# Pads between buffers: every main matmul's moving operand 288 bytes past its weights, modulo 512

## The reference

```python
for l in range(DEPTH):
    h = hybrid_mixer(x, w_in[l], ...);            x = layer_norm(alpha * x + h, ...)
    h = memory_cross_attention(x, mem, ...);      x = layer_norm(alpha * x + h, ...)
    h = conv_ffn(x, ffn_w_in[l], ...);            x = layer_norm(alpha * x + h, ...)
```

## Time and profile before

| | |
|---|---|
| Median of 3 runs | 2807.03 us (2804.65 to 2807.98) |
| Profiled execution | 2804.18 us |
| Its span, first to last instruction | 2802.4 us |
| TensorE busy (PE), weight loads (PEld) | 2721.5 us, 2499.1 us |
| VectorE, ScalarE, GpSimd busy | 2108.0 us, 1693.9 us, 71.8 us |
| Read from HBM | 675.32 MB, 243 GB/s over the span |
| Mean granted TensorE clock | 0.987 of full speed |

### The profile page before, as it was taken

How to read it: one execution, slowest core, us unless ns; L and a number is a source line. 1 busy time by engine, 2 the same in 40 slices (tenths; PEclk the granted TensorE clock), 3 DMA queues, 4 the chain that set the end, 5 groups by cost and what they waited for, 6 DMA issues and landing times.

```text
span 2802.4 us, 42816 instructions
## 1 busy us (share of the span) xinstructions
PE 2721.5 (97%) x18410; PEld 2499.1 (89%) x18418; DVE 2108.0 (75%) x2088; ACT 1693.9 (60%) x1856; POOL 71.8 (3%) x114
## 2 busy tenths in 40 slices
PE   7999999999999999999999999999999999999998
PEld 6999999999999989989999999888888888888886
DVE  5777647876667658767577667688898989888896
ACT  4555536654555546645577654677777777677675
POOL 1100000001000000000000000000000000000000
PEclk9999999999999999999999989999999999999999
DMA  7545447745536457634588733698988989898894
GB/s 237 170 147 166 154 159 257 268 141 170 157 121 196 151 181 268 229 96 136 187 296 299 256 93 106 244 371 339 379 340 339 377 344 372 335 382 338 340 373 182
DMA packets 304403, 679.22 MB, mean 242 GB/s; under 512 B 16560, under 2 KB 238032, under 8 KB 261072
## 3 DMA queue, kind: packets, MB, share of 16 engines
q1 hardware_dynamic: 288832, 617.67, 61.5%
q0 software_dynamic: 15376, 58.75, 6.4%
HBM read 675.32 MB, written 4.69 MB: 243 GB/s over the span
## 4 chain that ended last, share of the span: by engine, by line
PE 79%; DVE 10%; ACT 8%; issue 2%; DMA 1%; SPq 0%; ACTq 0%; DVEq 0%
PE bank L550 75%; DVE ew_lo L1871 4%; ACT ring_tail L2058 3%; ACT w_hi L1989 2%; DVE ring_low L1362 1%; PE bank L1166 1%; DMA ring_head<-in_w_in 1%; PE bank L630 1%; DVE std L1295 1%; PE bank L590 1%; DVE ring_tail L1319 0%; DVE ring_low L1282 0%; PE bank L669 0%; DVE xT L1616 0%; ACT ew_hi L2342 0%
## 5 line engine op out<-in xcount | busy, mean ns | idle before, releaser
L1871 DVE TENSOR_TENSOR ew_lo<-ring_head,ew_hi 128x2048 fp32r<-128x2048 f32 x336 | 759.3, 2287 | 41.5 <-ACT ew_hi L2342 41.5
L2342 ACT CAST ew_hi<-ring_head 128x2048 fp32r<-128x2048 f32 x336 | 640.6, 1915 | 223.9 <-PE bank L550 223.8
L550 PE MATMUL bank<-xs_hi,ring_low 128*128 128x256 f32 (+1 forms) x2608 | 511.9, 283 | 0.0
L550 PEld LDWEIGHTS bank<-xs_hi,ring_low 128*128 128x128 f32 (+1 forms) x2608 | 414.1, 190 | 1.5 <-issue 0.7
L550 PE MATMUL bank<-ew_hi,xe_hi 128*128 128x512 f32 x896 | 353.2, 394 | 0.0
L550 PE MATMUL bank<-ew_hi,xe_lo 128*128 128x512 f32 x896 | 349.3, 390 | 0.0
L550 PE MATMUL bank<-ew_lo,xe_hi 128*128 128x512 f32 x896 | 348.7, 389 | 0.0
L550 PE MATMUL bank<-x_hi,w_hi 128*128 128x256 f32 x1152 | 322.0, 287 | 13.5 <-ACT x_hi L2050 7.7
L550 PE MATMUL bank<-x_hi,ring_low 128*128 128x256 f32 x1152 | 316.6, 281 | 0.0
L1362 DVE TENSOR_TENSOR ring_low<-ring_head,w_hi 128x2048 fp32r<-128x2048 f32 x105 | 240.0, 2289 | 101.1 <-ACT w_hi L1989 101.1
L550 PE MATMUL bank<-x_lo,w_hi 128*128 128x256 f32 x1080 | 296.9, 281 | 0.0
(11 more groups left out here) (430 smaller groups left out, 5497.7 us busy)
## 6 DMA issues: line engine op xcount, KB each, us to landing
ring_head<-in_moe_w_gate SPq DMA_DIRECT2D x112, 1024.0 KB, 7.2
ring_head<-in_moe_w_up SPq DMA_DIRECT2D x112, 1024.0 KB, 7.0
ring_head<-in_moe_w_down SPq DMA_DIRECT2D x112, 1024.0 KB, 7.1
ring_head<-in_w_in SPq DMA_DIRECT2D x82, 1024.0 KB, 5.4
ring_tail<-in_ada_w POOLq DMA_DIRECT2D x48, 1024.0 KB, 10.0
ring_head<-in_ffn_w_in SPq DMA_DIRECT2D x44, 1024.0 KB, 6.4
ring_head<-in_ffn_w_out SPq DMA_DIRECT2D x22, 1024.0 KB, 8.7
ring_head<-in_xa_kv SPq DMA_DIRECT2D x16, 1024.0 KB, 5.4
```

What stands on the lines that cost most here:

```text
L550: ins = nc.tensor.matmul(out, lhsT, rhs, start=start, stop=stop, **kw)
L1871: v.tensor_tensor(ew_lo[:, h, :], ring(c % 6), ew_hi[:, h, :].bitcast(F32), ALU.subtract).then_inc(w_used[c % 6], 1)
L2342: a.copy(ew_hi[:, (e * len(PARTS) + c) % DEPTH_HI, :], ring(c % 6)).then_inc(f.count(part_hi), 1)
```

## The change

Eight pads are declared between buffers, `SKEW` = 56 floats (224 bytes) or `SKEW_BACK` = 72 floats (288 bytes). No instruction, no size and no order changes. The starts modulo 512 become:

| Buffer | before | after |
|---|---|---|
| ring_low, ring_head, xT, work, memT, ye, back, kb, gates | 128 | 128 |
| xs_hi, xs_lo | 416 | 416 |
| chunk_high | 416 | 128 |
| qa, qb, hc, mem, out (high and low), mixer buffers | 416 | 416 |
| w_hi | 416 | 128 |
| x_hi, x_lo, act_hi, act_lo | 416 | 416 |
| ew_hi, ew_lo | 416 | 416 |
| xe_hi, xe_lo, eact_hi, eact_lo | 416 | 128 |

```diff
--- before.py
+++ after.py
@@ -42,6 +42,7 @@
 MIXER_CHUNKS = 16
 NARROW = 40
 DT_AT = 32
+SKEW, SKEW_BACK = 56, 72
 class Follow:
 
 
@@ -204,26 +205,34 @@
         with ExitStack() as loads:
             with ExitStack() as twin:
                 xs = [in_scope(twin, n, KD, TOK, dt=F32R) for n in ("xs_hi", "xs_lo")]
+                skew_chunk = in_scope(twin, "skew_chunk", SKEW)
                 chunk_high = in_scope(twin, "chunk_high", CH, dt=F32R)
             ring_tail = in_scope(loads, "ring_tail", SLOTS - 6, CH)
+            skew_loads = in_scope(loads, "skew_loads", SKEW)
             with ExitStack() as twin:
+                skew_q = in_scope(twin, "skew_q", SKEW_BACK)
                 _, qb_hi, qb_lo, _, hc_hi, hc_lo, qa_hi, qa_lo = (in_scope(twin, n, k, TOK, dt=F32R) for n, k in (
                     ("under_q", 12), ("qb_hi", 4), ("qb_lo", 4), ("under_v", 12), ("hc_hi", 4), ("hc_lo", 4), ("qa_hi", 4), ("qa_lo", 4)))
             with ExitStack() as twin:
+                skew_mem = in_scope(twin, "skew_mem", SKEW_BACK)
                 _, mem_hi, mem_lo = (in_scope(twin, n, k, TOK, dt=F32R) for n, k in (("under_mem", 32), ("mem_hi", KD), ("mem_lo", KD)))
             with ExitStack() as twin:
+                skew_out = in_scope(twin, "skew_out", SKEW_BACK)
                 _, out_hi, _, out_lo = (in_scope(twin, n, k, TOK, dt=F32R) for n, k in (
                     ("under_out", 44), ("out_hi", 4), ("between_out", 4), ("out_lo", 4)))
             with ExitStack() as mixer:
+                skew_mixer = in_scope(mixer, "skew_mixer", SKEW_BACK)
                 qa, ka, qb, gb, gc, hc = (in_scope(mixer, n, 4, TOK) for n in ("qa", "ka", "qb", "gb", "gc", "hc"))
                 va, vb = (in_scope(mixer, n, 2, 512) for n in ("va", "vb"))
                 qhalf = [[in_scope(mixer, f"qhalf{a}{m}", 4, TOK) for m in range(2)] for a in range(2)]
                 probsT = in_scope(mixer, "probsT", 2, 2, 2, TOK)
             with ExitStack() as ffns:
                 w_hi = in_scope(ffns, "w_hi", DEPTH_HI, CH, dt=F32R)
+                skew_x = in_scope(ffns, "skew_x", SKEW_BACK)
                 x_hi, x_lo = (in_scope(ffns, n, KD, TOK, dt=F32R) for n in ("x_hi", "x_lo"))
                 act_hi, act_lo = (in_scope(ffns, n, 2, 2, TOK, dt=F32R) for n in ("act_hi", "act_lo"))
         ew_hi, ew_lo = (sb(n, DEPTH_HI, CH, dt=F32R) for n in ("ew_hi", "ew_lo"))
+        skew_xe = sb("skew_xe", SKEW)
         xe_hi, xe_lo = (sb(n, KD, P, dt=F32R) for n in ("xe_hi", "xe_lo"))
         eact_hi, eact_lo = (sb(n, ETILES, P, dt=F32R) for n in ("eact_hi", "eact_lo"))
 
```

## The result

The changed kernel takes 2824.44 us (median of 4 runs, 2820.72 to 2827.03), the kernel before 2807.09 (4 runs, 2804.65 to 2807.98). The ratio is 1.0062, with a 95% interval of 1.0047 to 1.0077: slower by some 17 us, where 15 us faster was forecast, and outside the range of 2775 to 2806.

The account below looks back on a forecast made before the run. The prediction took a stream of TensorE matmuls, whose spacing sets the time, as the bound, except in the wide feed-forward. Gains of 3.2 + 1.7 + 10.5 = 15.4 us gave 2791.5 us as likeliest, range 2775 to 2806.

Parts of the forecast that it names:

- The chunks of 256 columns: Straight 256-column matmuls: mixed distances to all 288 saves 1.06 ns each; turned ring_low chunks keep 118.3 ns.
- Term 3: Experts: 4032 matmuls of 512 columns gain 3.2 ns each, 12.9 us, less 2.4 at changes of expert: 10.5 us.
- the rival that ended on the slower side: Experts: streams meet their weights later, 3.0 ns a matmul on top of today's pitch, 2814 us; chance 6%.
- 216 ns: Rival in the experts: matmuls fall to the pitch of bf16 products with unchanged weights, 2766 us; chance 12%.
- Term 1: Dense feed-forwards: 3168 matmuls gain 1.06 ns each, times 0.95, 3.2 us; the wide one gives nothing.
- The share of 0.95: TensorE's share of the chain in layer 1's dense feed-forward (94.7%), used to scale the gain of Term 1.
- Term 2: Mixers and cross attention, chunks with hi in chunk_high: 2016 matmuls gain 1.06 ns each, times 0.80, 1.7 us.
- VectorE and ScalarE: Their operations at the new addresses: VectorE's subtraction at no cost, ScalarE's casts put at nothing.

Follow-up runs that it names:

- e1: The changed kernel without its last pad, before xe, so the experts are back at distance 0: 2804.24 us, ratio 0.9992 to the kernel before.
- m1: Also m1_map: a kernel of its own, only groups of 48 fp32r matmuls at 89 settings; 512 columns took 226.9 ns at distance 0, 233.1 at 288.
- e2: The kernel before with the pad before xe alone (224 bytes): 2825.50 us, ratio 1.0078.
- e4: The kernel before with a pad of 256 bytes before xe: 2806.01 us, ratio 1.0005.
- e5: The kernel before with a pad of 192 bytes before xe (distance 64 modulo 256): 2813.00 us, ratio 1.0024.
- e3: The changed kernel with straight 256-column products at distance 192 modulo 256 and experts back at 0: 2792.20 us, ratio 0.9953 to the kernel before.
- e8: The same kernel as e3, measured once more: 2796.45 us, ratio 0.9966.
- e7: As e3, but the dense feed-forwards' w_hi, x and act lie as in the kernel before: 2796.33 us, ratio 0.9959.
- m3_map_columns: A kernel of its own, only matmul groups of 64 to 512 columns, narrower weights and bf16; 512 columns with 32-column weights: 11.11 us at 0, 10.89 at 32.

## Why the prediction was wrong, step by step

- **The chunks of 256 columns**: right in the rows above. From 116.8 and 117.9 ns to 116.6 in the chain, and the turned ones unchanged. Distance 32 is cheaper than 0 there, and that is not a property of the buffers. But 116.6 is one of two spacings: the changed kernel has stretches at 117.8 ns too, in the feed-forward of layer 2 from 1137 to 1157 us, and e1 has them through all of that feed-forward. The prediction took one row for the whole stage.
- **Term 3, the experts: the failed step.** It says "The excess hardly grows with the columns: it goes with the change of weights, once per matmul. So I take the same 3.2 ns". The first half was read at distance 0 alone, where it is true (13.3 and 13.8 ns), and carried over to a distance at which only 256 columns had been seen. There it is false: 10 ns at 256 columns, 20 at 512. The 3.2 ns gained became 6.2 ns lost: 4032 x 6.2 = 25.0 us, of which 21 show. The difference fits the wait at the change of expert: before, loads of weights waited 4.6 us in all for xT, seven times (the row below); after, that wait is gone. m1, e2, e4 and e5 show the term, alone and in the kernel, at distances 0, 288, 256 and 320 modulo 512.

```profile
PEld bank L1166 <- DVE xT L1616: 4.6, 7, 0.7
```

- **The pads were named modulo 512**; the period is 256. That changed nothing here, since both residues are 32 modulo 256, but the search has half the room.
- **The bounds.** No row offered a price above 227.1 ns at 512 columns, and the rival that ended on the slower side was priced from turned chunks, 3.0 ns on top of today's: 2814, at 6%. It was right in sign and in that the loss comes with the longer stream, had half the size (3.0 for 6.2 ns), and too small a chance; its mechanism is neither shown nor refuted. An unknown whose one end had no row above it deserved a range open upwards: 216 ns was taken seriously below, nothing as far above.
- **Term 1, the feed-forwards, 3.2 us:** at most 0.7 us came in layer 1, where it said 1.6, and nothing in layer 2. The share of 0.95 was read from the chain, which says who was last, not by how much. From the first to the last start of x_hi with w_hi, layer 1 takes 176.7 us before, 176.0 in the changed kernel, 176.7 in e1 with the same pads, 176.8 in e3; layer 2 takes 176.8 before and 177.0 in the changed kernel. These are layer 1's rows of before and of e3:

```profile
L550 PE MATMUL bank<-x_hi,w_hi x352: 278/281/551, 424.9 to 601.6; 128*128 128x256 f32 x176
```
```profile
L559 PE MATMUL bank<-x_hi,w_hi x352: 276/281/582, 422.1 to 598.9; 128*128 128x256 f32 x176
```

  Two things take the gain. One is waiting. TensorE's line had 94.7% of this stage; in the changed kernel, from 460 to 600 us, the casts, subtractions and folds of ScalarE and VectorE have most of the chain:

```profile
by line: PE bank L559 34.9%; DVE ring_low L1371 18.0%; ACT w_hi L1998 9.8%; issue 9.2%; DVE ring_tail L1328 5.7%; ACT ring_tail L2067 4.7%; DVE gates L1581 3.6%; DVE ring_tail L1330 3.5%; DVE gates L1585 3.2%; DVE gates L1589 3.1%; DVE gate
```

  In e3 TensorE is busy for 137.5 of these 140 us, where before it was for all 140. The other is the second spacing, at which e8's matmuls gain nothing on those of before. How much falls on each is not separated. The wide feed-forward, put at nothing, kept its length as forecast: 236.4 us before, 236.5 after. (It lasts to about 1626 us, not to 1580.)
- **Term 2, the mixers, 1.7 us:** 1.6 us at the start of the experts, but e1 with the same pads has them start 0.6 us later than before; at this size it can't be told. That mixers do pay for pitch is shown by e3 and e7.
- **VectorE and ScalarE** at new addresses: unchanged (ew_lo 2286 against 2287 ns, ew_hi 1912 against 1915).
- **The rule of the Trainium skill** ("TensorE: Matmul & The Clock Gate", Part 2, "Step-by-step: what each phase is for"), by which loading weights takes nothing from the running matmul: bf16 agrees (109 ns at 256 columns at all three distances tried), fp32r does not, by up to 16 ns a matmul in these maps (226.7 to 243 at 512 columns).

What stays open is the law itself. Why 512 columns want 0 and 256 want 192, why one setting has two spacings and what makes a stream in the full kernel take one or the other, and what exactly the two reads share, no run here settles; that the clash lies within TensorE's reads of fp32r operands, with period 256 bytes, is shown.

## What to carry to other kernels

A stream that costs more than its columns may owe it to where its operands lie; a kernel of nothing but matmuls shows it, and the best place has to be measured for each width, since the one for 256 columns was among the bad ones for 512. Don't carry a cost from one shape to another on the strength of one setting in which both agree. And a chain of waits that runs 95% through one engine doesn't say that a faster engine is repaid: here waits for two other engines, and a second, dearer spacing of the same matmuls, took what a cheaper pitch gave, while a dearer pitch was paid in full. So look at the pitch through the whole stage, not in one row.

## What the runs showed of the hardware that was not expected

- fp32r matmuls: pitch by distance modulo 256 bytes, 113.3 to 120.6 ns at 256 columns and 226.7 to 243.3 at 512; a step of 4 bytes can move it by 12 ns (11.68 us for 48 at 100 bytes, 11.09 at 104).
- The lowest pitches found, 113.3 and 226.7 ns, are 272 and 544 cycles of 2.4 GHz: 16 cycles over the columns for each 256. bf16 with the same loads of weights settles at 109.2 and 215.8 ns at distances 0, 32 and 192.
- One setting may run at either of two steady spacings (256 columns: 113.3 or 117.8 ns at distance 192, 116.7 or 117.8 at 32), by what ran before it; in the full kernel it changed behind a wait.
- 128, 192 and 224 columns cost the same at the 2.4 GHz level: 5.36 us for 48, 111.7 ns, each with its own 128 x 128 weights (m1_map, m3_map_columns).
